# Copies of the last attention head's six results on VectorE instead of ScalarE

## The reference, cut to what matters

```python
o_cmp, p_cmp = compressed_attention(q, kc, vc, scale)      # branch 0: 63 compressed keys
o_slc = selected_attention(q, k_s, v_s, sel_idx, scale)    # branch 1: causal, all 16 blocks are selected
o_win = window_attention(q, k_w, v_w, scale)               # branch 2: causal, window of 512
o_attn = g3[..., 0:1] * o_cmp + g3[..., 1:2] * o_slc + g3[..., 2:3] * o_win
o_attn = o_attn.reshape(b, s_len, ATTN_WIDTH) * jax.nn.silu(z_attn)
merged = (jax.nn.sigmoid(m_a) * (o_attn @ w_proj_attn[l])
          + jax.nn.sigmoid(m_s) * (o_ssm @ w_proj_ssm[l]))
x = x + gate * (merged @ w_out[l])
return rms_norm(x, final_gain)
```

## Time and profile before

| | us |
|---|---|
| median of 3 runs | 935.35 |
| lowest and highest | 935.31, 936.28 |
| the profiled execution | 936.38 |
| its span, first to last instruction | 934.50 |
| PE busy | 895.4 (96%) |
| DVE busy | 524.5 (56%) |
| ACT busy | 416.6 (45%) |
| POOL busy | 205.9 (22%) |

### The profile page before, as it was taken

How to read it: one execution, slowest core, us unless ns; L and a number is a source line. 1 busy time by engine, 2 the same in 40 slices (tenths; PEclk the granted TensorE clock), 3 DMA queues, 4 the chain that set the end, 5 groups by cost and what they waited for, 6 DMA issues and landing times. The chain is left out here.

```text
span 934.5 us, 14430 instructions
## 1 busy us (share of the span) xinstructions
PE 895.4 (96%) x5577; PEld 737.8 (79%) x5577; DVE 524.5 (56%) x1096; ACT 416.6 (45%) x828; POOL 205.9 (22%) x203
## 2 busy tenths in 40 slices
PE   2899999999999999999999999999999999999997
PEld 2578999789999777777777776888888888887885
DVE  3652374359665697797797796732222122237454
ACT  5742232522345478778778768721111111133221
POOL 3369812111000103213212212254640000000000
PEclk9999999999999999999999999999999999999998
DMA  9956042041010000000000001333232111134222
GB/s 301 331 155 95 6 116 69 1 95 46 1 47 1 1 1 1 1 1 1 1 1 1 2 1 35 85 97 107 62 107 53 43 52 40 57 123 136 90 91 90
DMA packets 61092, 59.46 MB, mean 64 GB/s; under 512 B 10240, under 2 KB 53824, under 8 KB 61008
## 3 DMA queue, kind: packets, MB, share of 16 engines
q1 hardware_dynamic: 58768, 53.90, 20.2%
q0 software_dynamic: 2000, 4.54, 1.7%
q10 hardware_dynamic: 256, 0.09, 0.0%
HBM read 52.69 MB, written 5.24 MB: 62 GB/s over the span
## 5 line engine op out<-in xcount | busy, mean ns | idle before, releaser
L1236 DVE TENSOR_TENSOR plo<-pt,phi 128x512 fp32r<-128x512 f32 x192 | 109.5, 584 | 41.1 <-ACT phi L849 39.8
L849 ACT ACTIVATE pt<-bank 128x512 f32<-128x512 f32 (+1 forms) x208 | 99.3, 478 | 54.0 <-PE bank L1761 53.4
L1761 PE MATMUL bank<-q,k 128*128 128x512 f32 (+3 forms) x384 | 103.1, 350 | 0.0
L849 ACT ACTIVATE phi<-bank 128x512 fp32r<-128x512 f32 (+1 forms) x208 | 99.4, 478 | 0.0
L1761 PEld LDWEIGHTS bank<-q,k 128*128 128x128 f32 x384 | 63.6, 191 | 12.5 <-ACT phi L849 2.7
L648 POOL TENSOR_TENSOR qa<-qa,otmp 128x256 f32<-128x256 f32 x32 | 27.1, 846 | 204.3 <-DVE otmp L1236 204.3
L1554 DVE TENSOR_REDUCE mx<-slc_max 128x1 f32<-128x128 f32 (+3 forms) x64 | 48.2, 753 | 11.1 <-PE slc_max L1761 9.3
L1761 PE MATMUL bank<-ht_hi,dhi 128*128 128x512 f32 x128 | 49.8, 389 | 0.0
L1761 PE MATMUL bank<-ht_lo,dhi 128*128 128x512 f32 x128 | 49.8, 389 | 0.0
L1761 PE MATMUL bank<-ht_hi,dlo 128*128 128x512 f32 x128 | 49.8, 389 | 0.0
L1761 PE MATMUL bank<-phi,vhi 128*65 128x512 f32 (+3 forms) x128 | 45.9, 358 | 1.2 <-ACT osb L849 0.9
(11 more groups left out here) (444 smaller groups left out, 2596.6 us busy)
## 6 DMA issues: line engine op xcount, KB each, us to landing
ada<-in_w_ada SPq DMA_DIRECT2D x16, 512.0 KB, 10.1
draw<-in_w_in SPq DMA_DIRECT2D x16, 512.0 KB, 4.0
wraw<-in_w_in SPq DMA_DIRECT2D x7, 1024.0 KB, 5.3
xs<-in_x SPq DMA_DIRECT2D x8, 512.0 KB, 8.3
gstage<-in_w_ada POOLq DMA_DIRECT2D x16, 256.0 KB, 3.0
oraw<-in_w_out SPq DMA_DIRECT2D x8, 512.0 KB, 6.5
xr<-in_x SPq DMA_DIRECT2D x8, 512.0 KB, 4.3
out<-yr SPq DMA_DIRECT2D x7, 512.0 KB, 2.9
```

Of the source, the lines that this page charges most:

```text
L849: return nc.scalar.activation(o, i, fn, **kw)
L1236: return V.tensor_tensor(o, a, b, op)
L1761: return T.matmul(o, l, r, start=start, stop=stop, **kw)
```

## The change

ACT no longer copies the results of the last head. In the walk over the plan its condition now asks for a head before the last. DVE's branch for `V` steps, which so far did one thing (the weights of the last unit), takes every `V` step of the last head and copies the accumulator where a branch and half is complete. It waits for the copy before (`osb`), for the product (`pv`) and for the transposes of the buffer it overwrites (`ot`). PE, POOL and SP have the same instructions in the same order.

```diff
@@ block.scalar
                 elif step[0] == "V":
                     e = step[1]
                     br, cc, j = units[e % NU][0:3]
-                    if e % NU + 1 == NU or units[e % NU + 1][0:2] != (br, cc):
+                    if e // NU < HEADS - 1 and (e % NU + 1 == NU or units[e % NU + 1][0:2] != (br, cc)):
@@ block.vector
-                elif step[0] == "V" and step[1] == HEADS * NU - LAG:
-                    weights_low(HEADS * NU - 1)
+                elif step[0] == "V" and step[1] // NU == HEADS - 1:
+                    e = step[1]
+                    if e == HEADS * NU - LAG:
+                        weights_low(HEADS * NU - 1)
+                    br, cc = units[e % NU][0:2]
+                    if e % NU + 1 == NU or units[e % NU + 1][0:2] != (br, cc):
+                        n = 6 * (e // NU) + 2 * br + cc
+                        dve.wait_ge(once("osb"), n)
+                        dve.wait_ge(once("pv"), e + 1)
+                        dve.wait_ge(once("ot"), n - 1)
+                        V.tensor_copy(osb[n % 2][:, :], acc_bank(n)[0:HD + 1, :]).then_inc(once("osb"), 1)
```

## The result

The changed kernel takes 937.87 us (median of 17 runs, 936.98 to 939.55), the kernel before in the same session 935.37 us (17 runs, 935.03 to 937.84). The two medians lie 2.50 us apart. The ratio estimated from all runs is 1.0021 with a 95% interval of 1.0014 to 1.0027, that is 2.0 us slower, between 1.3 and 2.5. The forecast was 937.2, with 935.9 to 938.4 as its range. A second set of 11 runs gave 937.71 us and a ratio of 1.0019 (1.0011 to 1.0028).

The account below looks back on a forecast made before the run. PE was taken to bound the kernel, with no gap from 603 to 837 us to recover lateness. Terms 0.80 + 0 + 0.28 + 0 + 0.85 = 1.93 us on the 935.35 median gave 937.2 us, range 935.9 to 938.4.

Parts of the forecast that it names:

- What bounds: PE, without a gap from 603 to 837 us, cannot catch up lateness; relieving ACT's exponentials counted as 0 us.
- Price of a copy: DVE copy 0.69 us against ACT's 0.59, next instruction after 0.61; PE starts 0.16 us after DVE, 0.05 after ACT.
- Results 42 and 43: Two DVE copies ahead of `lsum` of result 41 delay `otmp`, bank 7 and PE's transposes of result 42: +0.80 us.
- Result 44: DVE's copy lets PE start 0.20 us sooner, eaten by slower copy and handover: 0.00 us.
- Result 45: DVE's copy stands behind weights; PE starts at 584.66 us instead of 584.38: +0.28 us.
- Result 46: Copy ends about 589.00 us, before PE wants it at 589.47, and POOL's addition does not hold it: 0.00 us.
- rival C: POOL's addition blocks copy 46 (+0.25) and a copy's three waits cost DVE +0.4: 2.6 us, 937.9; chance 15%.
- Result 47: DVE's copy stands behind `dlo`, so the transposes of result 47 and the gate products come later: +0.85 us.
- A (relief): DVE is at hand when products 44 and 45 end; both `osb` waits vanish (-0.93 us): 934.4; chance 5%.
- B (only the end counts): Bank 7 chain finds slack before the transposes of result 42, leaving 0.85 + 0.28 = 1.1 us: 936.5; chance 19%.
- D: The built order of instructions differs from the text; chance 1%.
- E: DVE's copy runs at twice the rate, 0.43 us, for a total of 0.6 us: 936.0; chance 3%.

Follow-up runs that it names:

- e3: Kernel before, with only results 44 and 45 copied by VectorE, the other four by ScalarE: 936.09 us against 935.63, ratio 1.0005; last head +0.06 us.
- e2: Kernel before, with only results 42 and 43 copied by VectorE, the other four by ScalarE: 936.28 us against 935.63, ratio 1.0009; last head +0.68 us.
- e7: Changed kernel, with VectorE copying result 47 ahead of `dlo`: 936.78 us against 936.02 for the kernel before, ratio 1.0006.
- e4: Kernel before, all copies on ScalarE, last-head results alternating between bank 6 and the second half of `slc_max`: 934.50 us against 935.63, ratio 0.9989.
- e6: Changed kernel, with VectorE copying result 43 behind `otmp` of result 41: 937.22 us against 936.02 for the kernel before, ratio 1.0012.
- e9: The changed kernel run once more, unaltered, against the kernel before: 937.71 us against 935.45, ratio 1.0019; last head 28.28 us.
- e10: Kernel before with ScalarE copies and alternating accumulators in the last head, run again: 934.88 us against 935.45, ratio 0.9990.

## Why the prediction was right

The direction and the places were right, and so was the mechanism: a copy costs what the work ahead of it in DVE's queue keeps PE waiting. The sum of 1.93 us was too large by 0.43 against the head. That it lies so close to the 2.0 us of the ratio is partly luck, for the ratio holds some of the scatter of the executions and the head doesn't.

- **What bounds.** Right: PE without a gap from 603 to 837, the rest of the kernel constant at 338.6 us, and no wait of PE for ACT's exponentials before or after. That ACT's relief is worth nothing by itself no run isolates; in the changed kernel `phi` of unit 186 is ready 0.49 us earlier (0.78 us after the zero, 1.27 before), but DVE comes to it only at 2.26.
- **Price of a copy.** 0.69 forecast, 0.68 measured; the next instruction begins 0.60 us after it (570.15 to 570.75). The handover was mis-sized: taken as 0.16 us from a row of transposes that waited for `qa`, it is 0.06 after a copy (575.49 to 575.55, 596.73 to 596.79), and stays 0.15 after `otmp` and `qa` (571.95 to 572.10, 574.06 to 574.21).
- **Results 42 and 43.** Forecast +0.80, measured +0.63 at the transposes of 42 and +0.56 at those of 43 (5.45 and 4.89 us after the zero). `lsum` moved by 1.05 us as worked out (1.09). The step that was off is the 1.32 us from `lsum` to the end of `otmp`, carried over from before: it is 1.20, since weights 186, which had waited for ACT's exponentials, were ready by then. A chain that starts later finds its other inputs there.
- **Result 44.** Forecast 0.00, measured -0.02 (6.79 - 5.45 against 6.25 - 4.89).
- **Result 45.** Forecast +0.28, measured +0.14 (9.17 against 9.03 us between the two starts). The 0.10 of the handover and the copy's 0.01 explain most of it. That the wait stays, with DVE as releaser, was right.
- **Result 46.** Forecast 0, measured +0.04, and rival C's reason for more (POOL holding the copy) was wrong: 0.68 us beside POOL's addition.
- **Result 47.** Forecast +0.85, measured +0.78; the copy stood behind `dlo` as laid out. Here too the handover made the difference.
- **Rivals.** A (relief) is refuted by e3: copies 44 and 45 alone give no gain, they cost 0.06 us. B (only the end counts) is refuted by e2. D fell too: the profile has the six copies on DVE, in the places named. C's other half, 0.1 us for the three waits of a copy, isn't there: a copy follows the instruction ahead of it by about 0.6 us behind 512 columns and at once behind the held weights, as weights do. E fell with 0.68 us.
- **The line of 0.2%.** The forecast lay on it, and so does the measured ratio (1.0021, with 1.0014 and 1.0027 as bounds); the head alone (1.50 us, 0.16%) lies under it.

## What to carry to other kernels

Moving work to the engine with less to do helps only if it is at hand at that moment: ask what stands ahead of the work in the other engine's queue and what that waits for, not how busy the engine is. Two copies ahead of a chain that ends just in time cost 0.68 us where one cost 0.08, and a copy behind a long instruction cost 0.81. Where an engine waits for a buffer to be emptied, another buffer (here an accumulator that is free at these places of the last head) took the wait away and gave 1.3 us; beginning copy 44 0.2 us earlier, on DVE (e3, 5.40 and not 5.60 us after the zero), gave 0.1.

## What the runs showed of the hardware that I had not expected

- VectorE's copy of 65x512 fp32 out of PSUM beside a GpSimd addition took 0.68 us, as alone; the subtraction with both operands in SBUF, beside POOL, took 1.35 and 0.98 us for 0.69 and 0.42. Both fit what the Trainium skill, SBUF — State Buffer, "Who interferes with whom", states: a DVE instruction with at most one SBUF input does not contend with GpSimd, one with two contends with a GpSimd instruction that reads SBUF.
- PE began 0.06 us after a DVE copy ended, products and transposes alike, but 0.15 us after a DVE multiplication or subtraction: the transposes after `otmp` and `qa`, and in e7 the gate product after `dlo` (595.97 to 596.12). In these rows the difference goes with DVE's instruction, not with PE's; why is not shown. It should be read from a row of the same kind.
- The idle time in brackets on PE understates a wait by the overlap of neighbouring products in the profile (0.17 and 0.19 us at the two places); e4 gained 1.32 us where the brackets showed 0.93. A row without a bracket can hide a wait: in e6 PE was 0.33 us late at result 45 and its row shows none.
- In the profiles the scatter between executions lay in the first 329 us (2.8 us); the remaining 606 us of one kernel repeated within about 0.1 us (the changed kernel and e9, e4 and e10). Up to 1.0 us of it arose before 322 us, and 0.9 to 2.8 us in the 7 of 12 profiles in which the granted clock fell to 0.50 after PE's wait of 2.24 us.
